# Row tiles scaled on VectorE and turned by transposes, another place for small buffers, weight pieces made earlier, and no drains in row stages

## The chip, the cores and the metric

The kernel runs on one core of a Trainium2 chip, as a single launch. The metric is the device time in microseconds; the time before is the median of three runs, 2115.38 us (2114.04 to 2116.16).

## The reference, cut to what matters

A sequence of 512 positions with 1024 features goes through two blocks. Everything is float32. The first block has a sparse attention, a retention and an MLP with a squared ReLU. The second has two layers. Each of these is, with rms for `x * rsqrt(mean(x*x) + eps)`:

```
h = rms(x) * w_pre
y = mixer(h)                     # mLSTM in layer 0, forgetting attention in layer 1
x = x + rms(y) * w_post          # after each mixer
h = rms(x) * w_ffn_pre
u = causal_conv3(h @ w_up) ; gate, val = split(u)
y = (gelu(gate) * val) @ w_down  # w_down: 2816 x 1024, so 22 tiles of 128 rows
x = x + rms(y) * w_ffn_post
```

After layer 0 keys, values and forget gates for layer 1 are made from x (`shared_kv`).

## The kernel before, in words

Activations lie transposed: x is `xT`, eight tiles of 128 features by 512 positions. Each product of two float32 matrices is made of three matmuls (`three_products`, L428): each operand is split into a high and a low part, and high by high, high by low, low by high are added up in PSUM. The high part is a rounded copy by ScalarE (`hi_part`, L342; the copy is L363), the low part is the difference, by VectorE (`lo_part`, L365; L378).

Weights come in blocks of at most 128 x 2048 (1 MB). SyncE loads a block into one of two buffers `raw`, and its two parts go into one of two rings, `w_hi` and `w_lo`, by turns. One such block with its two parts is called a piece here. Piece b of a stage may be written once the products of the block that used the ring last are done: ScalarE waits for `products_done` in `hi_part`. In a row stage with a norm behind it the pieces of the stage are 0 to 3, and 4 and 5 are the first two of the next stage. Piece 4 has a place of its own, `spare_w`, in the fourth big buffer.

The program is a list of stages, and each engine runs its part of them in the order written; engines meet at semaphores only. There are two kinds of stage. In `dense` (L477) the weights are stationary and 512 positions of the activations move; output is transposed as the input. In a row stage the activations are stationary, 128 positions at a time, and 512 columns of weights move, so that the output has positions on the partitions. Plain row stages are `vg`, `rvg`, `mv`, `fv` and `fd00`, `fd01`, `fd10`, `fd11` (`dense_rows`, L602). The two halves q = 0, 1 of the inner dimension are two blocks, four row tiles t accumulate in four banks, and g counts the column groups. Behind each pair of blocks TensorE drains (L655) and then counts `products_done`. `rvg`, `mv` and `fv` run as loops on TensorE (L660). The stage `mo`, which is interleaved with the mLSTM, has drains of its own (L2444).

The down projection of the second block's FFN is cut into groups by `FG` (L104): 8, 8 and 6 tiles of 128 hidden features, with stages `fu00`, `fd00`, `fu01`, `fd01`, `fu02`, `fd02` in layer 0 and `fu10` to `fd12` in layer 1. `fu` stages are dense.

`rows_post` (L837) is a row stage with both norms behind it: `mout` and `fout` (the mixers' output projections; `add` is False) and `fd02` and `fd12` (`add` is True: the group's product is added to y). Column group 0 is computed for all four row tiles; then group 1 for row tiles 0 and 1, then for 2 and 3. For a row tile t VectorE takes the product (`take`, only with `add`), ScalarE squares it with a row sum (`square`, L958), VectorE multiplies it by the post gain (`gained`, L1039), ScalarE takes the root (`post_sqrt`, L965), VectorE updates x (`update`, L1044 to L1049); ScalarE squares x (`pre_sqrt`, L970) and takes the root of the mean.

Then x must be transposed and divided by its root. VectorE writes `diag`, the identity scaled with 1/root (`diagonal`, L1055), and TensorE multiplies x by it (`turn_rows`, L916), 32 matmuls of 128 x 128 for two row tiles. ScalarE and VectorE split what comes out into `a_hi` and `a_lo` (`high_pair`, `low_pair`), and the next stage computes its first two blocks for the first 256 positions (`by_half`, L536) while row tiles 2 and 3 are still being made. `block_free` (L1112) lets block n start on the banks once the last product of row tiles is out of them. The last stage, `fd12`, has no next one: its rows of x are stored by DMA (L1109).

The big buffers `big` (four, seen as `big_halves` where they are halves) hold among others the hidden activations of the FFN and of the MLP and the heads of `mout`. They, `conv`, the small buffers before them, and `shared` behind them are allocated in the order of the text, each rounded up to 32 bytes.

## Time and profile before

| | |
|---|---|
| median of three runs | 2115.38 us |
| the profiled execution | 2118.26 us |
| its span, first to last instruction | 2116.5 us |
| TensorE matmuls busy | 2067.9 us, 98%, x10208 |
| VectorE busy | 1193.2 us, 56% |
| ScalarE busy | 814.2 us, 38% |
| granted TensorE clock, mean | 0.995 |
| DMA | 190.68 MB, 24.9% of 16 engines on the main queue |

The page takes a matmul as busy until its modelled end, so 98% does not say that TensorE is at its peak: matmuls follow each other at 0.227 us or so and last 0.39. How fast they follow is read from their starts. In names, `bank<-w_hi,big_halves` has the moving operand first and then the stationary one.

### The profile page before, as it was taken

The page shows a single profiled execution, that of the slowest core. Times are in us where ns is not written, and L with a number is a line of the kernel's source. Part 1 is how long each engine was busy: PE and PEld are TensorE (multiplying, and loading weights), DVE is VectorE, ACT ScalarE, POOL GpSimd, SP SyncE. Part 2 cuts the span into 40 slices and gives each one's busy share as a digit, 9 for nine tenths or more (in the row PEclk, how much of TensorE's full clock was granted, in tenths as well). Part 3 has the DMA queues.
Part 4 walks back from the last instruction along what each step waited for, and adds up shares of the span by engine and source line. Part 5 has one row for each costly group of instructions (what it writes and reads, how often), then busy time and mean ns, then how long its engine had stood idle before and what let it go on. Part 6 is the DMA issues. An engine that isn't in the chain of part 4 may idle for free.

```text
span 2116.5 us, 26480 instructions
## 1 busy us (share of the span) xinstructions
PE 2067.9 (98%) x10208; PEld 1680.6 (79%) x10216; DVE 1193.2 (56%) x1714; ACT 814.2 (38%) x1325; POOL 19.4 (1%) x42
## 2 busy tenths in 40 slices
PE   8999999999999999999999999999999999999998
PEld 6876778888888888877888887878786688888786
DVE  5768635454435365456475473764426856647466
ACT  4248242232212133245443342443426844324233
POOL 1000000000000000000000000000000000000000
PEclk9999999999999999999999999999999999999999
DMA  5410412322222221321222222222221032222222
GB/s 181 168 40 2 135 54 99 109 85 97 97 100 100 100 98 72 111 90 59 90 100 89 90 99 100 84 88 88 94 105 40 2 110 80 99 90 92 97 89 80
DMA packets 37972, 190.68 MB, mean 90 GB/s; under 512 B 4456, under 2 KB 12808, under 8 KB 18256
## 3 DMA queue, kind: packets, MB, share of 16 engines
q1 hardware_dynamic: 36096, 183.34, 24.9%
q0 software_dynamic: 1568, 5.65, 1.1%
q8 instruction: 65, 1.06, 0.2%
q10 hardware_dynamic: 208, 0.33, 0.0%
q14 instruction: 35, 0.29, 0.0%
HBM read 184.64 MB, written 2.11 MB: 88 GB/s over the span
## 4 chain that ended last, share of the span: by engine, by line
PE 88%; DVE 4%; PEld 3%; ACT 2%; issue 2%; DVEq 1%; DMA 0%; PEldq 0%; SPq 0%; ACTq 0%
PE bank L430 25%; PE bank L432 24%; PE bank L431 24%; PE bank L1418 2%; PE bank L517 2%; PE bank L518 2%; PE bank L522 2%; PE bank L1388 1%; PE bank L1405 1%; PEld bank L432 1%; PEld bank L430 1%; PEld bank L431 1%; PE bank L916 1%; PE bank L2426 1%; DVE w_lo L378 1%
## 5 line engine op out<-in xcount | busy, mean ns | idle before, releaser
L363 ACT ACTIVATE w_hi<-w_raw 128x2048 fp32r<-128x2048 f32 (+3 forms) x168 | 308.0, 1833 | 759.4 <-PE bank L432 587.4
L430 PE MATMUL bank<-a_hi,w_hi 128*128 128x512 f32 (+1 forms) x1424 | 549.2, 386 | 8.3 <-issue 7.2
L432 PE MATMUL bank<-a_hi,w_lo 128*128 128x512 f32 (+1 forms) x1424 | 545.2, 383 | 0.0
L431 PE MATMUL bank<-a_lo,w_hi 128*128 128x512 f32 (+1 forms) x1424 | 545.0, 383 | 0.0
L378 DVE TENSOR_TENSOR w_lo<-w_raw,w_hi 128x2048 fp32r<-128x2048 f32 (+3 forms) x168 | 367.8, 2190 | 280.7 <-ACT w_hi L363 280.7
L430 PEld LDWEIGHTS bank<-a_hi,w_hi 128*128 128x128 f32 x1424 | 268.4, 188 | 63.4 <-issue 10.8
L432 PEld LDWEIGHTS bank<-a_hi,w_lo 128*128 128x128 f32 x1424 | 268.3, 188 | 52.7
L431 PEld LDWEIGHTS bank<-a_lo,w_hi 128*128 128x128 f32 x1424 | 268.5, 189 | 51.1
L430 PE MATMUL bank<-w_hi,big_halves 128*128 128x512 f32 x416 | 165.5, 398 | 1.0 <-issue 1.0
L431 PE MATMUL bank<-w_lo,big_halves 128*128 128x512 f32 x416 | 164.5, 395 | 0.0
L432 PE MATMUL bank<-w_hi,big_halves 128*128 128x512 f32 x416 | 164.4, 395 | 0.0
L430 PE MATMUL bank<-w_hi,a_hi 128*128 128x512 f32 (+1 forms) x352 | 136.4, 387 | 2.9 <-DVE big L1897 1.0
L432 PE MATMUL bank<-w_hi,a_lo 128*128 128x512 f32 (+1 forms) x352 | 133.9, 380 | 0.0
L431 PE MATMUL bank<-w_lo,a_hi 128*128 128x512 f32 (+1 forms) x352 | 133.9, 380 | 0.0
L430 PE MATMUL bank<-big_halves,w_hi 128*128 128x512 f32 x304 | 120.0, 395 | 0.1
L432 PE MATMUL bank<-big_halves,w_lo 128*128 128x512 f32 x304 | 119.2, 392 | 0.0
L431 PE MATMUL bank<-big_halves,w_hi 128*128 128x512 f32 x304 | 118.0, 388 | 0.0
L430 PEld LDWEIGHTS bank<-w_hi,big_halves 128*128 128x128 f32 x416 | 78.2, 188 | 21.6 <-issue 2.7
L432 PEld LDWEIGHTS bank<-w_hi,big_halves 128*128 128x128 f32 x416 | 78.2, 188 | 18.9
L431 PEld LDWEIGHTS bank<-w_lo,big_halves 128*128 128x128 f32 x416 | 78.2, 188 | 18.3
L430 PEld LDWEIGHTS bank<-w_hi,a_hi 128*128 128x128 f32 x352 | 66.1, 188 | 21.7 <-issue 7.3
L432 PEld LDWEIGHTS bank<-w_hi,a_lo 128*128 128x128 f32 x352 | 66.1, 188 | 12.7
(368 smaller groups left out, 2571.1 us busy)
## 6 DMA issues: line engine op xcount, KB each, us to landing
w_raw<-in_w_fu SPq DMA_DIRECT2D x44, 1024.0 KB, 4.8
w_raw<-in_w_up SPq DMA_DIRECT2D x16, 1024.0 KB, 4.8
w_raw<-in_w_down SPq DMA_DIRECT2D x16, 1024.0 KB, 4.8
w_raw<-in_w_fd SPq DMA_DIRECT2D x16, 1024.0 KB, 4.8
w_raw<-in_w_fd SPq DMA_DIRECT2D x8, 768.0 KB, 4.3
w_raw<-in_w_rqk SPq DMA_DIRECT2D x4, 1024.0 KB, 5.4
w_raw<-in_w_rvg SPq DMA_DIRECT2D x4, 1024.0 KB, 4.9
w_raw<-in_w_gate SPq DMA_DIRECT2D x4, 1024.0 KB, 4.8
```

Of the source, the lines that this page charges most:

```text
L363: act.activation(dst[0][:, cols], raw[slot][:, cols], ACT.Copy).then_inc(hi_half_ready.sem if half == 0 else hi_ready.sem, 1)
L378: ins = dve.tensor_tensor(dst[1][:, cols], raw[slot][:, cols], dst[0][:, cols].bitcast(F32), ALU.subtract)
L430: pe.matmul(out, w[0], x[0], start=first, stop=False)
L431: pe.matmul(out, w[0], x[1], start=False, stop=False)
L432: return pe.matmul(out, w[1], x[0], start=False, stop=last)
L517: pe.matmul(bank[2 * slot + c][:, :], w[0], x[0], start=k == 0, stop=False)
L518: pe.matmul(bank[2 * slot + c][:, :], w[1], x[0], start=False, stop=False)
L522: last = pe.matmul(bank[2 * slot + c][:, :], weights(ring, col)[0], x[1], start=False, stop=final)
L916: last = pe.matmul(turn_banks[p][:, col:col + P], xT[:, k, t * P:(t + 1) * P], diag[:, t * P:(t + 1) * P], start=True, stop=True)
L1388: pe.matmul(out[e][:, 0:w], q[a][half[e], i * P:w], k[b][half[e], 0:w], start=a == 0 and b == 0, stop=False)
L1405: last = pe.transpose(turn_bank[e][:, j * P:(j + 1) * P], prob(u, e)[:, j * P:(j + 1) * P], ident)
L1418: last = pe.matmul(out[rows, j * P:S], vals[:, j, rows], turned_keys(p, e, j), start=j == 0 and not (together and p == 1), stop=j == TT - ...
```

## The change

`FG` becomes 6, 8 and 8 tiles. `y_squares` and `x_squares`, two small buffers, are allocated behind `shared` and no longer before `conv`. In row stages the last row tile's matmul counts `products_done` itself, the drains and the loops on TensorE are gone, and the readers of the last row tile wait for `products_done`. `rows_post` with `add` gets a third place for the parts of piece 3, `third_w` in `a_lo`, whose writer waits only for the stage before; pieces 4 and 5 are made before the first squares (ScalarE) and around the takes and gains of group 0 (VectorE). `diagonal` becomes `normalize`: it multiplies the whole row tile of x by 1/root into `work4`, and `turn_rows` transposes that with the identity. In the stages with a next one, `square(1,2)` writes its unused output into `turn_banks[3]`, and the turns wait for it. On VectorE the low half of piece 5 and `update(2)` move from behind `low_pair(0)` to ahead of it. The Sqrt table is asked for before piece 3.

```diff
--- before.py
+++ after.py
@@ -101,7 +101,7 @@
 self.packed = packed
-FG = [(0, 8), (8, 8), (16, 6)]
+FG = [(0, 6), (6, 8), (14, 8)]
 def weight_forms():
@@ -218,7 +218,6 @@
 inv_col = sb(top, "inv_col", [P, TT])
 post_col = sb(top, "post_col", [P, TT])
 part_col = sb(top, "part_col", [P, TT])
-y_squares, x_squares = sb(top, "y_squares", [P, 2, TT]), sb(top, "x_squares", [P, TT])
 conv = sb(top, "conv", [P, 4, 88])
@@ -242,6 +241,7 @@
 neg_max, row_sum = ([sb(top, f"{n}{r}", [P, 2]) for r in range(3)] for n in ("neg_max", "row_sum"))
 ret_ssq, ret_root = (sb(top, n, [P, RH, TT]) for n in ("ret_ssq", "ret_root"))
 one = sb(top, "one", [P, 1])
+y_squares, x_squares = sb(top, "y_squares", [P, 2, TT]), sb(top, "x_squares", [P, TT])
 def big_tiles(i, first=0, tiles=KT, dt=F32):
     src = big[i] if dt == F32 else big_halves[i]
...
@@ -299,11 +299,15 @@
 stream = {"slot": 0, "turn": 0}
 spare_w = [big_halves[3][:, n * SLOT:(n + 1) * SLOT] for n in range(2)]
+third_w = [a_lo[:, 4 * n:4 * n + 4, :].rearrange("p k s -> p (k s)") for n in range(2)]
+
 def ring_of(spec, nxt, b, slot, m):
     if isinstance(b, int) and b == (spec.blocks if m["eager"] else 0) and (m["eager"] or m["crossed"]):
         return spare_w
-    turn = 1 if m["eager"] and isinstance(b, int) and b > spec.blocks else 0
+    if m["third"] and isinstance(b, int) and b == 3:
+        return third_w
+    turn = 1 if m["eager"] and not m["third"] and isinstance(b, int) and b > spec.blocks else 0
     return [x[(slot + m["turn"] + turn) % 2] for x in (w_hi, w_lo)]
 def load(eng, spec, b, slot, q):
@@ -358,7 +362,10 @@
     if dst is not spare_w:
         early = isinstance(b, int) and (b == spec.blocks + 1 or (m["crossed"] and b == 2))
-        act.wait_ge(products_done.sem, m["prod"] + b - (2 if early else 1))
+        if m["third"] and b in (3, 5):
+            act.wait_ge(products_done.sem, m["prod"] + b - 3)
+        else:
+            act.wait_ge(products_done.sem, m["prod"] + b - (2 if early else 1))
     cols = columns_of(n, half)
     act.activation(dst[0][:, cols], raw[slot][:, cols], ACT.Copy).then_inc(hi_half_ready.sem if half == 0 else hi_ready.sem, 1)
...
@@ -613,7 +620,10 @@
             g = (b - 1) // 2 if isinstance(b, int) else m["i"]
             for t in range(TT):
-                eng.wait_ge(rows_done.sem, m["rows"] + g * TT + (t + 1))
+                if t < TT - 1:
+                    eng.wait_ge(rows_done.sem, m["rows"] + g * (TT - 1) + t + 1)
+                else:
+                    eng.wait_ge(products_done.sem, m["prod"] + 2 * g + 2)
                 fn(eng, g, t).then_inc(rows_out.sem, 1)
         return early
...
@@ -645,24 +653,16 @@
                     w = [ring[(slot + m["turn"]) % 2][:, k * width:(k + 1) * width] for ring in (w_hi, w_lo)]
                     last = three_products(pe, bank[4 + t][:, 0:width], x, w, q == 0 and k == 0,
                                           q == 1 and k == tiles - 1)
-                if q == 1:
+                if t == TT - 1:
+                    last.then_inc(products_done.sem, 1)
+                elif q == 1:
                     last.then_inc(rows_done.sem, 1)
-                elif t == TT - 1:
-                    last.then_inc(products_done.sem, 1)
                 if between and (b, t) in between:
                     between[b, t](pe)
-            if q == 1:
-                pe.drain().then_inc(products_done.sem, 1)
-        if spec.blocks == 2 or between or tile_ready is not None:
-            for b in range(spec.blocks):
-                use(b, b % 2)
-        else:
-            with pe.Fori(0, spec.blocks // 2) as i:
-                m["i"] = i
-                use(i * 2, 0)
-                use(i * 2 + 1, 1)
+        for b in range(spec.blocks):
+            use(b, b % 2)
     finish(spec)
-    rows_done.n += TT * spec.blocks // 2
+    rows_done.n += (TT - 1) * spec.blocks // 2
     rows_out.n += TT * spec.blocks // 2
     return {"sync": sync, "scalar": scalar, "vector": vector, "tensor": tensor}
@@ -842,7 +842,7 @@
     spec, nxt, m = specs[name], after(name), marks()
-    m["eager"] = True
+    m["eager"], m["third"] = True, add
     final = pre is None
     per = spec.forms[0][0]
     slot0 = m["slot"]
@@ -851,10 +851,10 @@
     first_banks = [bank[low_bank + t] for t in range(TT)]
     second_banks = [bank[high_bank + 2 * ((slot0 + t // 2) % 2) + t % 2] for t in range(TT)]
     turn_banks = first_banks
-    diag = work4[:, 3, :]
+    normed = [work4[:, 2 * n:2 * n + 2, :].rearrange("p r (k j) -> p (r k) j", j=P) for n in range(2)]
     b_rd, b_gr = rows_done.n, gain_row_in.n
     b_yt, b_ys, b_yg, b_pr = y_taken.n, y_squared.n, y_gained.n, post_rooted.n
-    b_xu, b_rr, b_dg, b_rt, b_pk = x_updated.n, pre_rooted.n, diag_ready.n, rows_turned.n, plain_kept.n
+    b_xu, b_rr, b_xn, b_rt, b_pk = x_updated.n, pre_rooted.n, x_normed.n, rows_turned.n, plain_kept.n
     b_hi, b_lo, b_xt, b_xc, b_st = split_hi_done.n, split_lo_done.n, x_turned.n, x_copied.n, stored.n
     def y_done(eng, g, t):
@@ -880,7 +880,7 @@
             load(sp, nxt, 1, (slot0 + 1) % 2, 0)
     def ring(b):
-        return [x[(slot0 + b + m["turn"]) % 2] for x in (w_hi, w_lo)]
+        return third_w if add and b == 3 else [x[(slot0 + b + m["turn"]) % 2] for x in (w_hi, w_lo)]
     def products(pe, out, w, n, x, t, first, last):
         w = [r[:, n * 512:(n + 1) * 512] for r in w]
@@ -904,7 +904,9 @@
     def turn_rows(pe, pair):
         for t in (2 * pair, 2 * pair + 1):
-            pe.wait_ge(diag_ready.sem, b_dg + t + 1)
+            pe.wait_ge(x_normed.sem, b_xn + t + 1)
+        if pair == 0:
+            pe.wait_ge(y_squared.sem, b_ys + TT + 3)
         for p in range(4):
             if pair:
                 pe.wait_ge(split_lo_done.sem, b_lo + order.index(2 * p + 1) + 1)
@@ -913,8 +915,7 @@
             for k in (2 * p, 2 * p + 1):
                 for t in (2 * pair, 2 * pair + 1):
                     col = (k % 2) * 2 * P + (t % 2) * P
-                    last = pe.matmul(turn_banks[p][:, col:col + P], xT[:, k, t * P:(t + 1) * P], diag[:, t * P:(t + 1) * P],
-                                     start=True, stop=True)
+                    last = pe.transpose(turn_banks[p][:, col:col + P], normed[t % 2][:, k, :], ident)
             last.then_inc(rows_turned.sem, 1)
     def tensor(pe):
@@ -955,7 +956,8 @@
             y_done(act, g, t)
         if g or t:
             act.wait_ge(y_squared.sem, b_ys + TT * g + t)
-        act.activation(as_tiles(work4[:, 0, :]), source(g, t), ACT.Square,
+        unused = turn_banks[3] if g == 1 and t == 2 and not final else work4[:, 2, :]
+        act.activation(as_tiles(unused), source(g, t), ACT.Square,
                        accum_out=y_squares[:, g, t:t + 1]).then_inc(y_squared.sem, 1)
     def post_sqrt(act, t):
...
@@ -994,11 +996,15 @@
         if turn_x:
             copy_x_rows(act, 0)
             copy_x_rows(act, 1)
+        act.activation(warm[:, :], one[:, :], ACT.Sqrt)
         part(3)
-        act.activation(warm[:, :], one[:, :], ACT.Sqrt)
+        if add:
+            part(4)
+            part(5)
         for t in range(TT):
             square(act, 0, t)
-        part(4)
+        if not add:
+            part(4)
         square(act, 1, 0)
         post_sqrt(act, 0)
         square(act, 1, 1)
@@ -1006,6 +1012,7 @@
         if not final:
             pre_sqrt(act, 0)
             pre_sqrt(act, 1)
+        if not add:
             part(5)
         square(act, 1, 2)
         post_sqrt(act, 2)
@@ -1048,11 +1055,11 @@
             x = rows_of(xT, t, g)
             dve.scalar_tensor_tensor(x, rows_of(y, t, g), post_col[:, t:t + 1], x, ALU.mult, ALU.add).then_inc(x_updated.sem, 1)
-    def diagonal(dve, t):
+    def normalize(dve, t):
         dve.wait_ge(pre_rooted.sem, b_rr + t + 1)
         dve.reciprocal(inv_col[:, t:t + 1], inv_col[:, t:t + 1])
         dve.drain()
-        dve.tensor_scalar(diag[:, t * P:(t + 1) * P], ident, inv_col[:, t:t + 1], None, ALU.mult).then_inc(diag_ready.sem, 1)
+        dve.tensor_scalar(normed[t % 2], rows_of(xT, t), inv_col[:, t:t + 1], None, ALU.mult).then_inc(x_normed.sem, 1)
     def low_pair(dve, pair):
         for i, k in enumerate(order):
@@ -1067,37 +1074,39 @@
         ahead_dve(dve, lambda: part(1))
         part(2)
         part(3)
+        if add:
+            part(4)
         for t in range(TT):
             take(dve, 0, t)
         dve.wait_ge(gain_row_in.sem, b_gr + 16)
         for t in range(TT):
             gained(dve, 0, t)
         dve.tensor_scalar(part_col[:, :], y_squares[:, 0, :], 1.0 / D, EPS, ALU.mult, ALU.add).then_inc(post_rooted.sem, 1)
-        part(4)
+        part(5 if add else 4)
         for t in range(2):
             take(dve, 1, t)
             gained(dve, 1, t)
             update(dve, t)
         if not final:
-            diagonal(dve, 0)
-            diagonal(dve, 1)
+            normalize(dve, 0)
+            normalize(dve, 1)
+        if not add:
+            part(5)
         take(dve, 1, 2)
         gained(dve, 1, 2)
+        update(dve, 2)
         if final:
-            update(dve, 2)
             take(dve, 1, 3)
             gained(dve, 1, 3)
             update(dve, 3)
     def next_dve(dve, part):
         low_pair(dve, 0)
-        lo_part(dve, spec, nxt, 5, 1, m)
-        update(dve, 2)
         take(dve, 1, 3)
         gained(dve, 1, 3)
         update(dve, 3)
-        diagonal(dve, 2)
-        diagonal(dve, 3)
+        normalize(dve, 2)
+        normalize(dve, 3)
         low_pair(dve, 1)
         part(None, 2)
@@ -1117,7 +1126,8 @@
     def halves_in(pair, i):
         return (split_hi_done.sem, b_hi + KT * pair + i + 1), (split_lo_done.sem, b_lo + KT * pair + i + 1)
     finish(spec)
-    stream["turn"] = 1 - stream["turn"]
+    if not add:
+        stream["turn"] = 1 - stream["turn"]
     rows_done.n += TT - 1
     gain_row_in.n += 16
     post_rooted.n += 1 + TT
...
@@ -2438,10 +2448,10 @@
             x = [a[:, 4 * q + k, t * P:(t + 1) * P] for a in (a_hi, a_lo)]
             w = [ring[(slot + m["turn"]) % 2][:, k * 512:(k + 1) * 512] for ring in (w_hi, w_lo)]
             last = three_products(pe, bank[s][:, :], x, w, q == 0 and k == 0, q == 1 and k == 3)
-        if q == 1:
+        if t == TT - 1:
+            last.then_inc(products_done.sem, 1)
+        elif q == 1:
             last.then_inc(rows_done.sem, 1)
-        if tp == 1 and s == 1:
-            pe.drain().then_inc(products_done.sem, 1)
     def turn(pe, n):
         pe.wait_ge(head_gated.sem, b_hg + n + 1)
...
```

## Rows read from the trace of the kernel before

**Rows 1.** The page, part 4: chain that ended last, shares of the span by engine.

```profile
PE 88%; DVE 4%; PEld 3%; ACT 2%; issue 2%; DVEq 1%; DMA 0%; PEldq 0%; SPq 0%; ACTq 0%
```

**Rows 2.** Waits of PE: waiting line, releaser: us in total, times, longest us.

```profile
PE bank L430 <- issue: 8.7, 14, 1.7
```

**Rows 3.** Timeline of PE behind `mout`: start us, us, engine, line, names, count.

```profile
1046.32 0.28 PE L432 MATMUL bank<-a_hi,big_halves 128*128 128x256 f32 x1
...
1048.30 0.35 PE L430 MATMUL bank<-a_hi,w_hi 128*128 128x256 f32 x1 [1.70 <-issue]
```

**Rows 4.** Timeline of DVE in the same stretch.

```profile
1043.66 2.28 DVE L378 TENSOR_TENSOR w_lo<-w_raw,w_hi 128x2048 fp32r<-128x2048 f32 x1
...
1047.41 0.68 DVE L1039 TENSOR_TENSOR big<-bank,gain_row 128x512 f32<-128x512 f32 x1
```

**Rows 5.** Timeline of DVE and PE in `fd02`.

```profile
1397.40 1.76 DVE L378 TENSOR_TENSOR w_lo<-w_raw,w_hi 128x1536 fp32r<-128x1536 f32 x1 [6.83 <-ACT w_hi L363]
...
1412.18 0.39 PE L432 MATMUL bank<-w_hi,big_halves 128*128 128x512 f32 x1
...
1416.12 0.29 DVE L1055 TENSOR_SCALAR work<-const_sb,inv_col 128x128 f32<-128x128 f32 x1
```

**Rows 6.** The chain in order of time: start us, us, what, pieces merged.

```profile
1003.27 1.75 PE bank L896 x16
...
1416.55 5.45 PE bank L916 x32
...
1749.16 3.58 PE bank L916 x32
```

**Rows 7.** Windows: stretch, us, busy by engine, PEclk (granted clock), DMA share, GB/s.

```profile
1416.50:1418.70 2.20, 2.15 (x14) 2.18 (x15) 0.92 (x2) 2.17 (x5) 0.00 (x0) 0.73 0.00 0
```

**Rows 8.** Source line 2543: count, duration ns min/median/max, first and last start.

```profile
L2543 DVE TENSOR_SCALAR big<-big x8: 417/420/428, 922.5 to 983.4; 128x512 f32<-128x512 f32 x8
```

**Rows 9.** Timeline of PE and DVE at the end of `fd12`.

```profile
2107.07 0.39 PE L432 MATMUL bank<-w_hi,big_halves 128*128 128x512 f32 x1
...
2112.06 1.42 DVE L1049 SCALAR_TENSOR_TENSOR xT<-big,post_col,xT 128x512 f32<-128x512 f32 x2
```

**Rows 10.** Timeline of PE and DVE at boundaries in `rvg`, `mv` and `fd00`.

```profile
234.76 2.72 DVE L1897 TENSOR_SCALAR big<-bank,inv_col 128x512 f32<-128x512 f32 x4
...
882.52 0.49 PE L430 MATMUL bank<-w_hi,a_hi 128*128 128x512 f32 x1 [0.72 <-DVE big L2305]
...
1134.00 0.39 PE L432 MATMUL bank<-a_hi,w_lo 128*128 128x512 f32 x1
...
1156.40 0.39 PE L432 MATMUL bank<-w_hi,big_halves 128*128 128x512 f32 x1
...
1157.05 0.47 PE L430 MATMUL bank<-w_hi,big_halves 128*128 128x512 f32 x1 [0.26 <-issue]
...
1179.29 0.40 PE L432 MATMUL bank<-w_hi,big_halves 128*128 128x512 f32 x1
...
1180.12 0.49 PE L430 MATMUL bank<-a_hi,w_hi 128*128 128x512 f32 x1 [0.44 <-issue]
```

**Rows 11.** Timeline of PE: first and last matmuls of unbroken runs.

```profile
500.69 0.40 PE L517 MATMUL bank<-big_halves,w_hi 128*128 128x512 f32 x1
...
544.43 0.39 PE L432 MATMUL bank<-big_halves,w_lo 128*128 128x512 f32 x1
...
1041.10 0.28 PE L431 MATMUL bank<-a_lo,big_halves 128*128 128x256 f32 x1
...
1054.01 0.28 PE L432 MATMUL bank<-a_hi,w_lo 128*128 128x256 f32 x1
...
1134.23 0.40 PE L430 MATMUL bank<-w_hi,big_halves 128*128 128x512 f32 x1
...
1689.43 0.40 PE L430 MATMUL bank<-w_hi,a_hi 128*128 128x512 f32 x1
...
1732.05 0.39 PE L432 MATMUL bank<-w_hi,a_lo 128*128 128x512 f32 x1
```

18 lines of the change are left out of this document (10 added, 8 removed).

## The prediction, made before the changed kernel was run

> **What bounds the kernel now.** The chain of waits comes first. In it the reader is to see TensorE carrying 88% of the path and VectorE 4% [rows 1]. So there are two sorts of gain: a matmul that starts sooner after the one before it, and the few places where VectorE holds TensorE up. The waits of TensorE name the second sort: fourteen idle stretches with no releaser, 8.7 us together, the longest 1.7 [rows 2]. The timeline says where the longest are: in the stage behind each of the row stages `mout`, `fd02` and `fout`, between block 0 and block 1 of the first half [rows 3]. Last I read steps from start to start in long unbroken runs of matmuls, since a matmul's recorded end is a model; every difference below is between two starts.
>
> **The ledger.** It is made against the profiled execution: 2118.26 us for a span of 2116.5, so 1.8 lie around the span and stay. The median of the three timed runs is 2115.38, 2.9 less; I take the sum off both.
>
> *Gap before block 1.* From 1046.32 to 1048.30 TensorE starts nothing: 1.98 us against some 0.2 for a restart [rows 3]. What it waits for is `block_free(1)`, the last `gained`. VectorE runs that at 1047.41 (0.68 us), because the low half of weight piece 5 (2.28) and `update(2)` (1.6) stand between `low_pair(0)` and it [rows 4]. The change puts both ahead of `low_pair(0)`. In `mout` VectorE is free from about 1031.4 and the high half of piece 5 is there at 1034.0, so the low half, `gained(1,2)` and `update(2)` end near 1038.7, before the first `a_hi` piece at 1039. `gained(1,3)` then ends near 1044.4, 2 us before it is needed. The other two gaps have the same build (none of the fourteen is over 1.7 by its idle time). Three times 1.77 is **5.3 us**; if VectorE were late by the same amount at another place it would be 0, and it can't be more.
>
> *The end of `fd02`.* Piece 3 waits for block 1 to finish. Its low half ends at 1399.1, 3.4 us after that block; all behind it on VectorE is late, and `diagonal(1)` ends at 1416.4. TensorE's last product starts at 1412.18 [rows 5], its turns at 1416.55 [rows 6]: 4.37 us. The 32 turns after this take 5.45 where they take 3.58 elsewhere [rows 6]. The granted clock shows why: 0.73 of full speed in the first 2.2 us of them [rows 7], so part of that stretch ran at 1.2 GHz and not at 2.4, after an engine idle for 4 us; after the idle 1.7 us of rows 3 it shows no fall. Now the stage has 8 tiles (21.8 us of products behind block 0's pair where 16.8 were), piece 3 goes to `a_lo` without waiting for block 1, and pieces 4 and 5 come early. With T the end of block 1: the low half of piece 2 is done at T-6.7, the gain row and the next stage's first megabyte are asked for then and land about 6.9 us later (my estimate from the present spacing), piece 4 is made from T+0.2 to T+4.4, the takes last to T+6.8, squares and `gained` to T+9.0, piece 5 to T+11.4, then 3.65 us go to each row tile (0.6 take, 0.8 square, 0.7 gained, 0.2 reciprocal, 1.4 update): tile 1 at T+18.7 and `normalize(1)` at about T+21. The products end at T+21.8. One wait is added: the turns wait for `square(1,2)`, whose scrap output now lies in `turn_banks[3]`. Behind it on TensorE stand the turns, and behind them the whole next stage. Tile 2 is finished at T+19.1, VectorE takes it after `normalize(1)`, the square ends at T+22.4: half a microsecond of wait stays. I take **3.6 us** of the wait (0 to 4.1) and **1.9** for the slow turns (0 to 1.9).
>
> *Scaling the tiles.* `normalize` treats 128x1024 where `diagonal` treated 128x128 in 0.29 [rows 5]. A TensorScalar over 512 in SBUF takes 0.42 [rows 8]; 1024 lies between that and the 1.4 of two updates. I take 0.7, so 0.4 more, twelve times. In `mout` and `fout` it lies under products (VectorE idle till 1034.8 in `mout`, turns at 1037.4). In `fd02` it is inside the T+21. Cost 0; without cover 0.4 to 1.1 for each tile on the path. The turns become transposes: 16 take 1.75 us where 16 of the old take 1.79 [rows 6]; 192 give **0.5 us**.
>
> *The final stage.* TensorE's last product starts at 2107.07, VectorE's last pair of updates ends at 2113.5 [rows 9]: 6.4 us, where one tile's chain with the completion is 4.0. VectorE has a backlog because piece 3 came late here too. Now it comes early and there are 8 tiles. Tile 2 is ready at T+19.4 and done at T+23.1, tile 3 is ready at T+22.1: a backlog of 1.0 stays. Gain **1.4 us** (0 to 2.4). The stores behind it (3.0) stay.
>
> *Drains.* In a dense row stage a drain stands behind every second block. In the middle of `fd00`, 1156.40 to 1157.05: 0.65, which with the long step behind it is 0.49 over two ordinary steps; at its end, 1179.29 to 1180.12, likewise 0.71 over. A boundary with neither drain nor wait, 1134.00 to 1134.23, costs nothing [rows 10]. If a satisfied wait leaves 0.1, it is 0.38 for each of four middles and 0.7 for each of four ends: 4.3. `mv` and `fv`, now loops, lose 0.9 each in the middle (for `mv` 0.72 idle before 882.52) [rows 10], though VectorE has emptied the first bank in time; with 0.5 and 0.3 at their ends, 2.6. `rvg` gets little: in its middle the first bank is emptied only from 234.76 [rows 10], VectorE being at the rotation till then, and that is what TensorE waited for; 0.6 for both its drains. `vg` 0.3. The four in `mo` I take at half a middle, 0.8. Together **8.6 us** (5, if the wait for a bank or the restart takes the drain's place, to 11). The loops of TensorE that are written out add no work.
>
> *The arena.* Small buffers are moved from before `conv` and the four big buffers to behind them. By the declared sizes, each rounded up to 32 bytes, the arena starts at byte 132,800 of a partition, 64 past a multiple of 128; the weight rings (16,512) and `a_hi` (82,048) are multiples of 128. Without the two buffers it starts at 132,736, a multiple of 128 and 99 x 512 bytes from `a_hi`. The trace has both cases side by side. Moving `w`, stationary tile in the arena: 95 steps from 1134.23 [rows 11] to 1156.40 [rows 10], 233.4 ns. The same form of stage with a stationary tile of `a_hi`: 188 steps, 226.7 ns. Moving operand in the arena, stationary `w`: 191 steps, 229.0 ns [rows 11]. If the offset is the cause, 1248 matmuls (22 tiles x 4 x 2 x 3 in each of two layers, 192 in `mout`) gain 6.7 ns, 8.3 us, and 1152 (`down`, `out1`, projections) 2.3 ns, 2.6 us. Against it: half-width products with their weights in the arena take 113.5 ns (46 steps to 1046.32), those with weights in the ring 119.9 (from 1048.30) [rows 3, 11]; if these become alike, 288 lose 6.4 ns, 1.8 us. Net **9.1 us**. The bounds are a gain of 10.9 and a loss that the third rival prices. I take the offset for the cause, since the two forms of stage differ in nothing else but the place in memory.
>
> Sum: 5.3 + 3.6 + 1.9 + 0.5 + 1.4 + 8.6 + 9.1 = 30.4. Profiled, 2118.3 - 30.4 = 2087.9; on the scale of the medians 2115.4 - 30.4 = **2085.0 us**.
>
> The order of the group sizes (6, 8, 8 for 8, 8, 6) moves work and adds none; its worth is in the two ends above. A short first block that ends before piece 1 is ready costs some 0.2 us; that moves from the last group to the first.
>
> **Rivals.** *The arena's place changes nothing* (27%). The slower step would then belong to the region, or to which buffers are read together. For it: the half-width rows go the other way within the same arena. Against it: same form of stage, same widths, same engine order. Time: 2085.0 + 9.1 = 2094.
>
> The Trainium skill, "Advanced Engine Details and Errata", section "Memory Cachelines", speaks for this rival: SBUF has lines of 16 bytes, and 64 is a multiple of 16, so by that rule both places are equal and the sum ends at 2094. The steps of 233.4 against 226.7 ns are not explained by it.
>
> *The row stages of `fd` stay late* (10%). Piece 4 now stands before the takes on VectorE, and it hangs on a transfer. If that lands 4 us later than I have it, `normalize(1)` ends at T+25, and the wait, the slow turns and the backlog at the end are all back. For it: the gain row and two megabytes share the queue there. Against: piece 3 no longer waits. Time: 2085.0 + 3.6 + 1.9 + 1.4 = 2092.
>
> *The new place is a worse one* (3%). As the half-width rows show, weights that lie like the ring's can be the slower ones, by 6.4 ns. If all 2400 matmuls met twice that, 12.8 ns, it would be 30.7 us lost where I count a gain, and the other six terms give 21.3: 2115.4 - 21.3 + 30.7 = 2125. It decides from 21.3 / 2400 = 8.9 ns per matmul; below that the others outweigh it.
>
> My forecast has the remaining 60%; its own range is 2081 to 2090. For 8 in 10: low end with drains at 11, the wait and the backlog gone and the half-width products unchanged, 2079; high end with the arena at nothing, drains at 5 and 3 us of another term missing, 2100. A difference of 0.2% is 4.2 us, about what a measurement of this kernel can tell from none. Only the third rival comes near that: faster 0.95, same 0.02, slower 0.03.
>
> **What the profile after would show.** No idle time before block 1 of the stage behind a row stage, and the last `gained` done before it; if the gap is there, VectorE's order has not helped. Turns in `fd02` within 1 us of the last product, all 32 in about 3.5. Boundaries in `fd` stages with a step under 0.35. Steps of 227 ns in long runs with stationary tiles from the arena; at 233 the first rival holds, above 240 the third. A last product some 5 us before the end of the last update. The forecast is wrong if TensorE waits over 2 us in `fd02`, or if the boundaries keep their half microsecond with the drains gone.

## The result, and the profile after

The changed kernel takes 2077.85 us (median of four runs, 2075.96 to 2079.51) where the kernel before takes 2115.77; the ratio is 0.9817, 95% interval 0.980 to 0.9835. The gain is 37.9 us, the forecast was 30.4: 2077.85 lies 1.15 us below the low end of the range. The profiled execution took 2079.51 us for a span of 2077.7.

The chain of waits (the page, shares of the span by engine) still ends in TensorE, with "issue" down to 1% [rows 1]:

```profile
PE 93%; DVE 4%; ACT 1%; DVEq 1%; issue 1%; DMA 1%; SPq 0%; ACTq 0%
```

The chain in order of time holds the first turn behind `mout` and the second (start us, us, what, records merged):

```profile
1029.84 1.75 PE bank L918 x16
1043.27 1.75 PE bank L918 x16
```

Before, such a turn had 32 records and took 3.58 [rows 6]. The loops in the code are the same, two row tiles by eight feature tiles: 16 instructions, and not the 32 that the text ahead of the prediction gives for a turn. The old form leaves two records in the trace for each, the new one leaves one. Most of the surplus over the forecast is here, as the first experiment shows.

The boundary between block 0 and block 1 behind `mout` (timeline of PE: start us, us, engine, line, names, count), which answers to [rows 3]:

```profile
1037.22 0.28 PE L439 MATMUL bank<-a_hi,big_halves 128*128 128x256 f32 x1
1037.34 0.28 PE L437 MATMUL bank<-a_hi,w_hi 128*128 128x256 f32 x1
```

A step of 0.12 us where there were 1.98. The stage `fd01`, first matmul, the middle and the first one behind it:

```profile
1220.19 0.39 PE L437 MATMUL bank<-w_hi,big_halves 128*128 128x512 f32 x1
...
1241.72 0.39 PE L439 MATMUL bank<-w_hi,big_halves 128*128 128x512 f32 x1
1241.95 0.39 PE L437 MATMUL bank<-w_hi,big_halves 128*128 128x512 f32 x1
...
1263.71 0.39 PE L437 MATMUL bank<-a_hi,w_hi 128*128 128x512 f32 x1
```

192 steps in 43.52 us are 226.7 ns, with no long step in the middle or at the end; [rows 10, 11] had 233.4 and two boundaries of 0.5 and 0.7 us over the ordinary.

The end of `fd02` (timeline of PE, then of DVE), against [rows 5]:

```profile
1394.04 0.39 PE L439 MATMUL bank<-a_lo,big_halves 128*128 128x512 f32 x1
1395.70 0.41 PE L918 MATMUL bank<-const_sb,work 128*128 128x128 f32 x2 [1.27 <-ACT bank L960]
...
1398.39 0.36 PE L437 MATMUL bank<-a_hi,big_halves 128*128 128x256 f32 x1 [0.75 <-DVE a_lo L1068]
```

```profile
1393.45 0.76 DVE L1062 TENSOR_SCALAR work<-xT,inv_col 128x1024 f32<-128x1024 f32 x1
1394.12 0.69 DVE L1042 TENSOR_TENSOR big<-bank,big 128x512 f32<-128x512 f32 x1
...
1396.43 1.42 DVE L1056 SCALAR_TENSOR_TENSOR xT<-big,post_col,xT 128x512 f32<-128x512 f32 x2
1397.76 3.22 DVE L1068 SCALAR_TENSOR_TENSOR a_lo<-bank,gains,a_hi 128x256 fp32r<-128x256 f32 x8
```

There are two waits. The turns start 1.66 us behind the last product, held by `square(1,2)`. Then `by_half` starts 1.02 us behind the last turn record, where some 0.2 is usual, so 0.8 late, held by `low_pair(0)` behind `update(2)`. From the last product to `by_half` it is 4.35 us; before it was 9.56 (1412.18 to 1421.74).

And the end of the kernel, against [rows 9]: 5.1 us from the last product's start to the end of the last update, where it was 6.4.

```profile
2069.62 0.39 PE L439 MATMUL bank<-a_lo,big_halves 128*128 128x512 f32 x1
```

```profile
2073.30 1.42 DVE L1056 SCALAR_TENSOR_TENSOR xT<-big,post_col,xT 128x512 f32<-128x512 f32 x2
```

### The profile page after: what moved, and what is told of

It reads as the page before. It is cut to its first block, busy times and chain, and to the rows that moved or that the text cites. A ratio compares the mean times of both kernels' runs of the same rounds, so it can differ in the third digit from the quotient of the medians.

```text
span 2077.7 us, 26174 instructions
## 1 busy us (share of the span) xinstructions
PE 2043.9 (98%) x10120; PEld 1670.0 (80%) x10120; DVE 1198.2 (58%) x1714; ACT 813.7 (39%) x1325; POOL 19.4 (1%) x42
## 4 chain that ended last, share of the span: by engine, by line
PE 93%; DVE 4%; ACT 1%; DVEq 1%; issue 1%; DMA 1%; SPq 0%; ACTq 0%
PE bank L437 26%; PE bank L439 26%; PE bank L438 26%; PE bank L1398 2%; PE bank L1428 2%; PE bank L524 2%; PE bank L529 2%; PE bank L525 2%; PE bank L1415 2%; PE bank L2436 1%; DVE w_lo L385 1%; ACT w_hi L370 1%; PE bank L2428 1%; PE bank L1649 0%; PE bank L1403 0%
## 5 line engine op out<-in xcount | busy, mean ns | idle before, releaser
L385 DVE TENSOR_TENSOR w_lo<-w_raw,w_hi 128x2048 fp32r<-128x2048 f32 (+3 forms) x166 | 363.4, 2189 | 258.5 <-ACT w_hi L370 258.5
L437 PE MATMUL bank<-w_hi,big_halves 128*128 128x512 f32 x384 | 150.3, 391 | 0.3 <-DVE w_lo L385 0.3
L439 PE MATMUL bank<-w_hi,big_halves 128*128 128x512 f32 x384 | 149.5, 389 | 0.0
L438 PE MATMUL bank<-w_lo,big_halves 128*128 128x512 f32 x384 | 149.5, 389 | 0.0
L437 PEld LDWEIGHTS bank<-w_hi,big_halves 128*128 128x128 f32 x384 | 72.1, 188 | 15.8 <-DVE w_lo L385 1.2
L439 PEld LDWEIGHTS bank<-w_hi,big_halves 128*128 128x128 f32 x384 | 72.1, 188 | 15.1
L438 PEld LDWEIGHTS bank<-w_lo,big_halves 128*128 128x128 f32 x384 | 72.1, 188 | 14.9
```

Of the source, the lines that this page charges most:

```text
L385: ins = dve.tensor_tensor(dst[1][:, cols], raw[slot][:, cols], dst[0][:, cols].bitcast(F32), ALU.subtract)
L437: pe.matmul(out, w[0], x[0], start=first, stop=False)
L438: pe.matmul(out, w[0], x[1], start=False, stop=False)
L439: return pe.matmul(out, w[1], x[0], start=False, stop=last)
```

## The experiments

Each was timed against the kernel before on the same chip, which had medians of 2115.2 to 2115.9 us there. Differences are between medians, against the control's 2076.86, unless a trace is named. Under some 2 us medians say little: the two traces of the changed kernel, the one above and the control's, differ by 1.9 us in the first 106 alone.

**The control.**

> The changed kernel again, nothing edited, as the mark for the other runs of this call. Every theory expects about 2077.9 us, 37.9 below the kernel before, and a profiled span near 2077.7.

Measured: 2076.86 us, span 2075.0. That is the mark for the others.

**The turn.**

```diff
-pe.transpose(turn_banks[p][:, col:col + P], normed[t % 2][:, k, :], ident)
+pe.matmul(turn_banks[p][:, col:col + P], xT[:, k, t * P:(t + 1) * P], diag[:, t * P:(t + 1) * P], ...)
-dve.tensor_scalar(normed[t % 2], rows_of(xT, t), inv_col[:, t:t + 1], None, ALU.mult)
+dve.tensor_scalar(diag[:, t * P:(t + 1) * P], ident, inv_col[:, t:t + 1], None, ALU.mult)
```

> The changed kernel, but x is turned again by matmuls against the scaled identity; the order of everything else stays. Theory one (the turn is the mis-sized term): the trace of before holds 192 records of 112 ns for these matmuls, the trace of after 96 records of 109 ns, for 96 instructions in either code. So each old turn of 16 instructions takes 3.58 us and each new one 1.75, and the run is 96 x (2 x 112 - 109) = 11.0 us slower than the changed kernel, less what a faster scaling (0.29 against 0.75 us on VectorE) gives back in the two stages where TensorE waits for it, at most 1.3: 9.7 to 11 slower, at 2087.6 to 2088.9 us. Rival (my term of 0.5 us was right and the surplus is elsewhere): 0.5 us slower, 2078.4. A third way, the longer turn lies under a wait for VectorE that ends later anyway: turns as long as before, but under 5 us in the sum.

The unused outputs of `square` and `pre_sqrt` go back to their old places in `work4` with it. Measured: 2087.96, 11.1 slower. In its chain the turns are long again:

```profile
1028.56 3.57 PE bank L918 x32
1043.65 3.57 PE bank L918 x32
```

Between starts, from the first record of a turn to the matmul behind it, it is 3.49 us against 1.78 to 1.84. In five turns that is 8.4 us, and in `fd02` 0.5 more, since TensorE waits there anyway. Between the two traces another 2.5 us lie in stretches that the edit leaves alone, 1.2 ahead of the first turn and 1.3 in the forgetting attention; so some 9 us is what the turns cost, and not all of the 11.1. Theory one holds, the rival is out, and so is the third way.

**The arena.** Seven kernels change only where buffers start, six of them made from the changed kernel and one from the kernel before. "Arena" is the stretch of the four big buffers. As the declared sizes give it, in the changed kernel the rings `w_hi` and `w_lo` start at byte 32,896 and 49,280 of a partition, `a_hi` and `a_lo` at 82,048 and 98,432, the arena at 132,736. (My prediction put the rings at 16,512; that is `raw`.) Each edit in one line, with what it moves:

```diff
 e_arena64, ahead of conv:  +y_squares, x_squares = ...        (arena + 64)
 b_arena, kernel before:    the same line moved behind one     (arena - 64)
 e_arena128, behind one:    +final_pre, warm, inv_col, post_col  (arena - 128)
 e_pad32, ahead of conv:    +sb(top, "pad", [P, 8])            (arena + 32)
 e_allshift, ahead of raw:  +sb(top, "pad", [P, 8])            (all + 32)
 e_ringrel, ahead of xT:    +sb(top, "pad", [P, 8])            (all behind the rings + 32)
 e_arena256, behind one:    +bias_b                            (arena - 256)
```

> The changed kernel with y_squares and x_squares ahead of conv again, so that the arena starts 64 bytes later in each partition; nothing else differs. Theory (the offset is the cause): the stationary-in-the-arena steps go from 226.8 back to 233.3 ns (1248 matmuls, 8.1 us), the moving-in-the-arena steps from 226.7 to 229.0 (1152, 2.7 us), the half-width products with weights in the arena from 120 to 115 (288, 1.5 us the other way): 9.3 us slower, 2087.2 us. Rival (something else in the change, the order of the groups or the loops that became straight code, made these steps shorter): the steps stay at 226.7 and the time at 2077.9.

> The kernel before with one edit, y_squares and x_squares allocated behind shared, so that the arena starts at 132,736 and not at 132,800. Theory (the offset is the cause, by itself): the steps with stationary tiles in the arena go from 233.4 to 226.8 ns, the moving ones from 229.0 to 226.7, the half-width ones from 113.5 to 120, 9 to 10 us faster than before (putting the offset back into the changed kernel cost 10.2 in the medians), at 2105.3 to 2106.3. A faster product stage can also show more of the wait for VectorE in fd02: then 8.5. Rival (the offset matters only with the new order of the stages): under 3 us.

Measured: 2087.08, 10.2 slower; and from the other side 2106.63, 9.3 faster than before. The steps moved as forecast, in both: in `e_arena64` from 226.7 ns to 233.4 with stationary tiles in the arena and to 229.0 with moving ones, in `b_arena` back to 226.7 to 227.9. So the place of the arena does it, with either order of the stages. But the rule that I had drawn from it fell with the next two:

> The changed kernel with four more small buffers behind shared, so that the arena starts at 132,608: still a multiple of 128, but its distance to the rings (32,896) and a_hi (82,048) is no longer a multiple of 512 or 256; it is 128 off. Theory A (what counts is the place against 128 bytes): steps of 226.7, no change, 2077. Theory B (what counts is the distance between the buffers that are read together, against 256 or 512): the long steps are back, 8 to 10 slower, 2085 to 2087.

> The changed kernel with 32 unused bytes ahead of conv, so that the arena starts at 132,768, 32 past a multiple of 128. Theory A (any offset against 128 costs the same, a row then touches one 128-byte stretch more): steps of 233.3 and 229.0 ns, 9 to 10 slower, 2086 to 2087. Theory B (it grows with the offset): half of it, steps near 230, 2082. Theory C (only 64 is bad): 2077.

Measured: 2090.21 (13.4 slower) and 2093.40 (16.5 slower). An arena that starts at a multiple of 128 bytes is worse than one 64 off. The last three tell place from distance:

> The changed kernel with 32 unused bytes ahead of the first buffer: rings, a_hi, arena and shared all start 32 bytes later, and the distances between them stay. Theory D (the distance between the two operands counts): steps of 226.7 ns everywhere, 2076.9. Theory P (an operand's own place counts): both sorts of steps of the arena are long as in e_pad32 (233.3), and those of a_hi with the rings too: 16 us slower or more, 2093 or above.

> The changed kernel with 32 unused bytes between the rings and xT: the rings stay, xT, a_hi, a_lo and the arena start 32 bytes later. Theory D (distance): the dense stages with a stationary tile of the ring and a_hi moving, 226.7 until now, go to 233 like the arena's, and the arena's stay long with the rings; only the pieces with both operands behind the gap (third_w with the arena) stay at 226.7. That is some 6.5 ns for each of about 8000 full-width products: 40 to 50 us slower, 2117 to 2127. Theory P (own place): the rings' own steps stay at 226.7 where they are stationary and cost only for the moved operand, as e_pad32: 16 to 30 slower.

> The changed kernel with one small buffer of 256 bytes (bias_b) behind shared: arena at 132,480, its distance to rings and a_hi a multiple of 256 but not of 512. Theory D256: 226.7 ns, no change, 2076.9. Theory D512: 232 to 233 ns in both sorts of steps, as with a distance of 128: 13 slower, 2090.

Measured: 2076.86, 2120.74 and 2077.52. The rows show 40 us out of each of up to three stages: a stage with stationary tiles in the arena (`fd01`), a dense stage with the ring against `a_hi` (`fu02`), and a dense stage that moves the arena past tiles of the ring (in the first block of the model). Columns as in [rows 7]; the count in PE's bracket is the number of matmuls in the 40 us. First the changed kernel, then `e_arena64`, `e_arena128`, `e_pad32`, `e_allshift`, `e_ringrel`, `e_arena256`:

```profile
1222.00:1262.00 40.00, 40.00 (x178) 33.14 (x177) 17.20 (x16) 8.82 (x6) 0.00 (x0) 1.00 0.30 106
1270.00:1310.00 40.00, 40.00 (x178) 33.11 (x178) 24.76 (x30) 16.51 (x18) 0.00 (x0) 1.00 0.28 103
500.00:540.00 40.00, 40.00 (x178) 33.13 (x177) 14.99 (x12) 8.12 (x5) 0.00 (x0) 1.00 0.29 106
```

```profile
1224.00:1264.00 40.00, 40.00 (x173) 32.22 (x172) 16.34 (x15) 8.82 (x6) 0.00 (x0) 1.00 0.30 103
1270.00:1310.00 40.00, 40.00 (x178) 33.13 (x177) 25.17 (x29) 13.78 (x15) 0.00 (x0) 1.00 0.31 105
500.00:540.00 40.00, 40.00 (x176) 32.81 (x176) 13.90 (x11) 6.96 (x4) 0.00 (x0) 1.00 0.30 105
```

```profile
1226.00:1266.00 40.00, 40.00 (x174) 32.44 (x173) 16.44 (x15) 8.82 (x6) 0.00 (x0) 1.00 0.29 102
...
500.00:540.00 40.00, 40.00 (x173) 32.16 (x173) 13.04 (x10) 5.78 (x4) 0.00 (x0) 1.00 0.29 105
```

```profile
1229.00:1269.00 40.00, 40.00 (x173) 32.20 (x172) 16.33 (x15) 8.81 (x6) 0.00 (x0) 1.00 0.29 103
...
500.00:540.00 40.00, 40.00 (x173) 32.15 (x172) 13.59 (x11) 6.65 (x4) 0.00 (x0) 1.00 0.29 105
```

```profile
1218.00:1258.00 40.00, 40.00 (x178) 33.13 (x177) 17.26 (x16) 8.98 (x7) 0.00 (x0) 1.00 0.30 106
```

```profile
1245.00:1285.00 40.00, 40.00 (x173) 32.21 (x172) 16.12 (x15) 8.68 (x6) 0.00 (x0) 1.00 0.30 106
1290.00:1330.00 40.00, 40.00 (x173) 32.11 (x172) 24.43 (x27) 13.76 (x15) 0.00 (x0) 1.00 0.30 105
```

```profile
1217.00:1257.00 40.00, 40.00 (x178) 33.15 (x177) 17.23 (x17) 9.14 (x7) 0.00 (x0) 1.00 0.31 105
```

The reader is to see 178, or 173 to 174. 178 is a step of 226.7 ns, 173 to 174 one of 232.4 to 233.4. With arena and rings a multiple of 256 bytes apart it is 178 (the changed kernel, `e_arena256`, and `e_allshift`, where every buffer lies 32 bytes further). At distances of 32, 64 and 128 it is 173 or 174, with one milder case, 176 (64, moving operand in the arena: 229.0). `e_ringrel` makes even the dense stages slow that read no tile of the arena: 43.9 us for 32 bytes of padding. In it the only fast full-width matmuls in `fd02` are those of the third ring place in `a_lo` with the arena, 227.7 ns, both behind the padding. So for products 512 wide it is the distance between the two operands that TensorE reads, modulo 256, as far as 32, 64, 128 and 256 can tell.

Products 256 wide do not follow this rule. With weights in the arena they take 121.4 ns at a distance of 0 or 256, 115 to 116 at 64, but 120 at 32 and at 128. With weights in the ring they take 120.0, and 116.7 in `e_ringrel`. Why, for either width, no run here shows.

The rule of the Trainium skill that my first rival rested on ("Advanced Engine Details and Errata", section "Memory Cachelines": lines of 16 bytes in SBUF) does not account for this; 32, 64 and 128 are all multiples of 16.

**The drains.**

```diff
-last.then_inc(products_done.sem, 1)
+pe.drain().then_inc(products_done.sem, 1)      # behind every second block, and in mo
```

> The changed kernel with the drains back, behind every second block of the plain row stages and in mo; products_done is counted by the drain. The loops on TensorE stay straight code. Theory (my ledger): 0.4 at each middle and 0.7 at each end, with the rest of my list: 8.6 us slower at most, 6 if the part of the loops (mv and fv, 1.8 in the middles) does not come back with straight code: 2084 to 2086.5. Rival (a wait takes the drain's place and the drain cost little): under 3 us slower, below 2081.

Measured: 2083.83, 7.0 slower. The middle and the end of its `fd01`:

```profile
1240.80 0.39 PE L439 MATMUL bank<-w_hi,big_halves 128*128 128x512 f32 x1
1241.42 0.47 PE L437 MATMUL bank<-w_hi,big_halves 128*128 128x512 f32 x1 [0.23 <-issue]
...
1263.06 0.39 PE L439 MATMUL bank<-w_hi,big_halves 128*128 128x512 f32 x1
1263.86 0.49 PE L437 MATMUL bank<-a_hi,w_hi 128*128 128x512 f32 x1 [0.41 <-issue]
```

With the long step behind each, that is 0.47 and 0.68 us over two ordinary steps; in the `fd01` of the changed kernel nothing is left of either. In the middle of `mv` drain and loop together cost 0.88 in the kernel before (a step of 1.107), the drain in straight code 0.40 here (0.623).

**VectorE's order.**

```diff
-update(dve, 2)                                   # ahead of low_pair(0)
 low_pair(0)
+if not add:
+    lo_part(dve, spec, nxt, 5, 1, m)
+update(dve, 2)
```

> The changed kernel with VectorE's old order behind the turns: update(2) in all four stages, and in mout and fout the low half of piece 5 too, stand behind low_pair(0) again. Theory: in mout and fout the last gained is again some 2 us late and TensorE waits before block 1, 1.8 us each; in fd02 only update(2) is moved, which lets low_pair(0) start 1.4 us sooner (the turns of the changed kernel are followed by 1.0 us of waiting for it), so that one stage gains 1.0 and may lose up to 0.5 before block 1. Sum 2.5 to 3.5 slower than the changed kernel's 2076.9: 2079.4 to 2080.4. Rival (my ledger's term, three full gaps): 5.3 slower, 2082.2.

Measured: 2078.71, 1.85 slower. The gap behind `mout`:

```profile
1034.13 0.28 PE L439 MATMUL bank<-a_hi,big_halves 128*128 128x256 f32 x1
1035.66 0.36 PE L437 MATMUL bank<-a_hi,w_hi 128*128 128x256 f32 x1 [1.25 <-issue]
```

That is 1.41 over a step, twice (`mout`, `fout`), less the 1.0 that `fd02` gains: 1.8. The mechanism is the one forecast; my expectation of 1.8 for each gap was 0.4 too much; 0.3 of that is that the 48 half-width products ahead of it last 121 ns each and not 115.

**What cures `fd02`.** Two edits could: the size of the group and the third place.

```diff
 e_nothird:
-m["eager"], m["third"] = True, add
+m["eager"], m["third"] = True, False             # parts 4 and 5 back at their old places
 e_fg:
-FG = [(0, 6), (6, 8), (14, 8)]
+FG = [(0, 8), (8, 8), (16, 6)]
```

> The changed kernel without the third place: piece 3 waits for block 1's products again and pieces 4 and 5 are made where they were; the groups stay 6, 8, 8. Theory one (the size of the group cures fd02, the third place is worth little): before, diagonal(1) ended 20.7 us after block 1 and the products 16.5 after it; with 8 tiles the products end 21.8 after it, and the longer low half and scaling put normalize(1) at 21.8 too. So the turns of fd02 start within 0.5 us of the last product; the gap before block 1 is back in fd02 (1.8), and the backlog of the last stage (up to 1.4): 2 to 3.5 slower, 2079 to 2080.5. Theory two (the third place carries it, as my ledger had it): the wait, the slow turns, the gap and the backlog are all back, 4.1 + 1.9 + 1.8 + 1.4 less 1.0 that the changed kernel still waits: 8 slower, 2085.

> The changed kernel with the groups 8, 8, 6 as before, all else kept. Theory one (the size of the group cures fd02): the products end 16.5 us after block 1, VectorE's chain, 21.7 in the changed kernel, shortens by 0.6 for each low half that has 3 in place of 4 tiles, so normalize(1) ends near 20.5 and TensorE waits about 4 us there; if it idles that long the clock falls and the turns take longer, some 1 us for 16 transposes; the last stage has 2 to 3 us more backlog: 6 to 8 slower, 2083 to 2085. Theory two (the third place carries it): under 1.5 us of waiting, 2077 to 2079.

Measured: 2081.03 (4.2 slower) and 2087.06 (10.2 slower). The times lie nearer to theory one in both, but both theories had the wait wrong. The turns of `fd02` in `e_nothird`, then in `e_fg`:

```profile
1390.19 0.39 PE L439 MATMUL bank<-w_hi,big_halves 128*128 128x512 f32 x1
1395.47 3.47 PE L918 MATMUL bank<-const_sb,work 128*128 128x128 f32 x16 [4.89 <-ACT bank L960]
```

```profile
1390.78 0.39 PE L439 MATMUL bank<-a_lo,big_halves 128*128 128x512 f32 x1
1399.94 0.45 PE L918 MATMUL bank<-const_sb,work 128*128 128x128 f32 x1 [8.77 <-ACT bank L960]
```

In `e_nothird`, VectorE ends `normalize(1)` 0.7 us after the last product, as theory one said; but the turns wait for `square(1,2)`, and its take stands behind the low half of piece 5:

```profile
1391.68 2.29 DVE L385 TENSOR_TENSOR w_lo<-w_raw,w_hi 128x2048 fp32r<-128x2048 f32 x1 [0.81 <-ACT w_hi L370]
1393.89 0.68 DVE L1038 TENSOR_TENSOR big<-bank,big 128x512 f32<-128x512 f32 x1
```

In `e_fg` the turns start 9.2 us after the last product, where the kernel before had 4.4 with the same groups. Counted from the end of block 1 the turns start at 21.2 us before, 25.5 in `e_fg`, 23.4 in the changed kernel and 27.0 in `e_nothird` (block 1's end taken as the last product less the 16.8, 16.3, 21.8 and 21.8 us that the products behind it last). So beside the long group the third place and the early pieces bring the turns 3.6 us forward; with the old groups the turns come 4.3 us later than before the change. 1.5 of these are the new wait for `square(1,2)`, from the end of `normalize(1)` to the turns. The rest is for the most part piece 4, which now stands ahead of the takes: they start 6.3 us behind block 1 in `e_fg` and started 3.7 behind it before. ScalarE waits for the transfer of piece 4 there, and VectorE for ScalarE:

```profile
1376.59 1.92 ACT L370 ACTIVATE big_halves<-w_raw 128x2048 fp32r<-128x2048 f32 x1 [4.29 <-DMA w_raw<-in_w_fk]
1378.54 2.29 DVE L385 TENSOR_TENSOR big_halves<-w_raw,big_halves 128x2048 fp32r<-128x2048 f32 x1 [4.44 <-ACT big_halves L370]
```

This is the prediction's second rival, the piece that hangs on a transfer. It holds with the old groups. The changed kernel has that wait too (VectorE idle for 5.61 us), but its products last 5.5 us longer and cover it. How much each of the moved pieces takes by itself no run shows. Each idle stretch also has its clock (windows of the turns, `e_nothird` and `e_fg`; the last three columns are PEclk, DMA share, GB/s):

```profile
1395.47:1398.70 3.23, 3.23 (x16) 3.23 (x17) 2.90 (x6) 1.53 (x4) 0.00 (x0) 0.51 0.71 294
```

```profile
1399.90:1402.90 3.00, 2.96 (x15) 2.99 (x16) 2.93 (x6) 1.30 (x4) 0.00 (x0) 0.53 0.00 0
```

This is close to the lower of the two levels, 1.2 GHz of 2.4: steps of 213 ns in place of 109, and turns of 3.0 to 3.2 us where 1.8 are usual.

**The two waits that are left.** `n_scratch` takes away only the turns' wait, in all three stages; `n_lowfirst` takes it away in `fd02` and also turns VectorE's order round there.

```diff
 n_scratch:
-if pair == 0:
-    pe.wait_ge(y_squared.sem, b_ys + TT + 3)
-unused = turn_banks[3] if g == 1 and t == 2 and not final else work4[:, 2, :]
+unused = total if g == 1 and t == 2 and not final else work4[:, 2, :]
 n_lowfirst, on VectorE, with add:
-gained(dve, 1, 2); update(dve, 2)                # ahead of low_pair(0)
 low_pair(0)
+gained(dve, 1, 2); update(dve, 2)
 and on ScalarE square(1,2), square(1,3) behind high_pair(0)
```

> The changed kernel, but square(1,2) writes its unused output to another buffer and the turns of fd02 no longer wait for it; VectorE's order stays. Theory (VectorE's order is what binds): the turns start 1.3 us sooner, right behind normalize(1), but low_pair(0) still stands behind update(2), which ends 3.4 us after normalize(1) started its last 0.75, so TensorE waits 2.3 us behind the turns where it waited 1.0: no change, 2076.9. Rival (the wait for the square is what costs): 1.3 us faster, 2075.6.

> The changed kernel, with one more edit in fd02: low_pair(0) stands ahead of gained(1,2) and update(2) on VectorE, both squares of group 1 for row tiles 2 and 3 behind high_pair(0) on ScalarE, and the turns do not wait for square(1,2). In the trace of the changed kernel the turns of fd02 start 1.66 us after the last product (1.27 of it idle) and are followed by 1.0 us of waiting for low_pair(0), since update(2) runs until 1397.84. Theory: both waits go, by_half starts 1.5 to 2.1 us sooner, and gained(1,3) is still in time, as 256 positions of two blocks last some 11 us: 2074.8 to 2075.4. Rival (the two gained and the late square now come too late for block 1): the gap before block 1 comes back and eats it, no change, 2076.9.

> The same kernel as n_lowfirst, a second time. In its first trace the stretch from the last product of fd02 to the first of by_half was 2.18 us against 4.26 to 4.35 in the changed kernel. Theory: 2.1 us faster than the changed kernel again, 2074.7 (its first median was 2074.4). Rival: that was the noise of the start-up, 2076.9.

Measured: `n_scratch` 2076.86, no change in the median. Its turns start 0.39 us behind the last product, and the wait has moved behind them:

```profile
1390.18 1.94 PE L916 MATMUL bank<-const_sb,work 128*128 128x128 f32 x16
1394.22 0.36 PE L437 MATMUL bank<-a_hi,big_halves 128*128 128x256 f32 x1 [2.10 <-DVE a_lo L1066]
```

And here the clock fell (windows from the start of `by_half`, columns as above):

```profile
1394.22:1396.22 2.00, 2.00 (x11) 2.00 (x12) 2.00 (x6) 2.00 (x6) 0.00 (x0) 0.65 0.00 0
1396.22:1398.20 1.98, 1.98 (x11) 1.98 (x11) 1.19 (x3) 1.98 (x6) 0.00 (x0) 0.50 0.00 0
```

The first 96 half-width products of `by_half` take 13.07 us where the control needs 11.58. From the last product of `fd02` to the second turn it is 17.50 us against 15.84: by its trace the edit is 1.7 us slower there. The median hides this; ahead of `fd02` this trace happens to be 1.7 us shorter than the control's.

`n_lowfirst` measured 2074.43, and 2075.94 the second time; ratios to before 0.9809 both times (0.9796 to 0.9822, 0.9794 to 0.9823), where the control has 0.9817 (0.9804 to 0.9831). In its trace both waits are gone:

```profile
1393.74 0.39 PE L439 MATMUL bank<-a_lo,big_halves 128*128 128x512 f32 x1
1394.12 1.94 PE L918 MATMUL bank<-const_sb,work 128*128 128x128 f32 x16
1395.92 0.36 PE L437 MATMUL bank<-a_hi,big_halves 128*128 128x256 f32 x1
```

It takes 2.18 us from the last product to `by_half`, 2.01 in the second run, against 4.26 in the control, and from that product to the kernel's last one 2.1 and 2.3 us less than in the control. So it is some 2 us better by its trace; the two medians, 2.4 and 0.9, allow it but the intervals overlap.

## Why the prediction was wrong, and where it was right

The step that failed is "The turns become transposes: 16 take 1.75 us where 16 of the old take 1.79 [rows 6]; 192 give **0.5 us**". Sixteen records are half of an old turn and a whole new one, and there are 96 instructions in six turns, not 192. I compared record with record and not turn with turn, although my rows had both whole turns in them: x16 in 1.75 and x32 in 3.58. Five turns gave 8.4 us in the trace, and with the old form back 8.9 returned by the trace and 11.1 by the medians. With some 9 us in the place of 0.5 the sum would have been 39, at 2076.5.

- *Gap before block 1*, 5.3: the three steps of 1.98, 1.98 and 1.79 us are 0.12 now, 5.4. Right, and the mechanism as well (`e_order`).
- *The end of `fd02`*, 3.6 and 1.9: last product to `by_half` went from 9.56 to 4.35, 5.2 us. That this is near the 5.5 is luck: the faster turn is in it with 1.7, so the waits and the slow clock gave 3.5. Half a microsecond was to stay; there stayed 1.4 ahead of the turns and 0.8 behind them, 1.27 and 0.75 of it idle, which just passes the 2 us at which the prediction calls itself wrong. Ahead of the turns the chain that I had added up was 0.5 us short: `square(1,2)` ends 22.9 us behind the recorded end of block 1 and not 22.4. Behind them I had not followed `update(2)`, moved ahead of `low_pair(0)` by the same change. That the clock would not fall was right (granted 1.00 in the turns). That piece 3's third place carries the term was not: it needs the longer group as well, since the turns start 9.2 us behind the last product without that group (`e_fg`) and 5.3 without the third place (`e_nothird`).
- *Scaling the tiles*: 0.75 us where I took 0.7.
- *The final stage*, 1.4: 1.3. The group's size is enough for it: from the last product to the end it is 8.06 us in the changed kernel and 8.07 without the third place, but 8.74 with the old groups and 9.39 before.
- *Drains*, 8.6: 7.0 in `e_drain`, with the loops left as straight code. In `mv` and `fv` 2.6 went, as forecast. In the `fd` stages all four middles and ends went, 0.49 and 0.71 each, 4.8 us where I had 4.3. Against this `fd00` and `fd10`, now of 6 tiles, have a step of 0.55 us and a long one behind it where block 0 ends: it waits for piece 1, whose low half ends at 1108.44, and costs 0.4 us, where the short `fd02` of before had 0.2. The middle of `rvg` still has its 1.43 us step, as forecast.
- *The arena*, 9.1: 9.3 and 10.2. The size was right, since it was read from rows of the same forms of stage; the reason was wrong. "A multiple of 128" fitted the two places that the trace of before showed. It took `e_arena128`, which keeps that and breaks the distance to the rings, to see it. That the new start is a multiple of 256 bytes from the rings as well was luck. The first rival (nothing) is out. The third (a worse place) is real, as `e_arena128` and `e_pad32` show, only not at this place.

Together, the arena by `b_arena` and the rest by the traces: 5.4 + 5.2 + 8.4 + 1.3 + 7 to 8 + 9.3 = 36.6 to 37.6, of 37.9. The terms are not quite independent: in `b_arena` the gaps before block 1 are up to 0.3 us shorter each, and the end of `fd02` is 1.4 longer, than in the kernel before.

## What to carry to other kernels

When a change swaps one form of an operation for another, count the records of one whole unit of work in both before comparing them; a record is not an instruction. Try the buffers that TensorE reads together at a multiple of 256 bytes apart, and check it by counting matmuls in a window: here 32 bytes of padding, far from most of the stages that it slowed, cost 2%. An edit that frees one wait is worth what the next in line leaves: `n_scratch` took 1.3 us off one and gave them all to the other, and behind the longer idle stretch the clock fell, which took 1.5 us more.

## What the runs showed of the hardware

- A float32 matmul of 128 columns against float32 weights takes two records and 218 ns (`e_diag`, 16 in 3.49 us), a transpose of the same tile one record and 109 ns (the changed kernel). The Trainium skill, "FP8 and Floating Point Precision", section "TensorE Precision Notes", says that true float32 takes four passes through the array; an estimate from that, with 128 columns at 2.4 GHz (53 ns), is 213 ns, so the trace agrees.
- The distance of the two operands modulo 256 bytes: for 512 columns 226.7 ns at 0, 232.4 to 233.4 at 32, 64 and 128, but 229.0 at 64 when the moving one lies in the arena. For 256 columns 120.0 to 121.4 ns at 0, and between 115 and 120 elsewhere, with no rule that these runs show.
- After 1.27 to 1.7 idle microseconds the granted clock stayed at full speed. After 2.10, behind 16 transposes, it was 0.65 in the mean of the next 2.0 us and 0.50 in the 2.0 after them (`n_scratch`). After 4.9 and 8.8 the following turns had 0.51 and 0.53, after 4.0 in the kernel before it was 0.73 in the first 2.2 us [rows 7].
